# Second mixer of a two-layer diffusion trunk: state sums and state products as three products of rounded halves, both scan directions merged into one mixing matrix

## The reference

```python
def ssd_chunk_scan(xs, dt, A, Bm, Cm, h0):       # L = 128 tokens a chunk, two chunks
    xdt = xs * dt;  a = dt * A
    def step(state, inp):
        xc, ac, bc, cc = inp
        cs = jnp.cumsum(ac, axis=1)
        seg = jnp.where(lower, cs[:, :, None] - cs[:, None, :], -jnp.inf)
        w = jnp.einsum('blgn,bsgn->blsg', cc, bc)[..., None] * jnp.exp(seg)
        y = jnp.einsum('blsgk,bsgkp->blgkp', w, xc)
        y = y + jnp.einsum('blgn,bgkpn->blgkp', cc, state) * jnp.exp(cs)[..., None]
        tail = jnp.exp(cs[:, -1:] - cs)[..., None]
        state = state * jnp.exp(cs[:, -1]) + jnp.einsum('bsgn,bsgkp->bgkpn', bc, xc * tail)
        return state, y

for d, rev in ((0, False), (1, True)):           # forwards and backwards
    yc_d, hc_d = ssd_chunk_scan(f(xc), f(dtc[:, :, d]), A[d], f(Bc), f(Cc), h0)   # context first
    yl_d, _ = ssd_chunk_scan(f(xl), f(dtl[:, :, d]), A[d], f(Bl), f(Cl), hc_d)    # then the latents
    yl = yl + f(yl_d)
```

## Time and profile before

| | us |
|---|---|
| median of 3 runs (lowest, highest) | 2140.7 (2139.47, 2143.54) |
| the profiled execution's own time | 2139.08 |
| its span | 2137.5 |
| PE busy | 2049.5 (96%) |
| DVE, ACT, POOL busy | 1438.1, 913.5, 776.6 |

### The profile page before, as it was taken

One profiled execution on the slowest core, in us unless ns is written; L12 is line 12 of the kernel. 1 busy time (PEld: TensorE's weight loads), 2 busy tenths in 40 slices (PEclk: granted clock), 3 DMA queues, 4 the chain that ended last, 5 costly groups with the idle time before them and its releaser, 6 DMA issues.

```text
span 2137.5 us, 31164 instructions
## 1 busy us (share of the span) xinstructions
PE 2049.5 (96%) x10694; PEld 1695.5 (79%) x10694; DVE 1438.1 (67%) x1865; ACT 913.5 (43%) x1259; POOL 776.6 (36%) x687
## 2 busy tenths in 40 slices
PE   5989999999999999989988999999999999999997
PEld 2558888888888888768867888888888888887776
DVE  5257777777787777744267767677767667678344
ACT  3244445444455455533354433433443434435433
POOL 1126666666665565645041221221322222222011
PEclk7999999999999999999989999999999999999999
DMA  9976666666676666445434455455454555544653
GB/s 352 361 218 143 184 162 170 171 175 176 174 189 171 169 174 171 137 133 152 111 106 123 127 138 148 118 137 149 106 162 113 142 141 134 127 133 167 239 194 138
DMA packets 417744, 349.21 MB, mean 163 GB/s; under 512 B 13504, under 2 KB 358176, under 8 KB 416544
## 3 DMA queue, kind: packets, MB, share of 16 engines
q1 hardware_dynamic: 392304, 269.76, 43.7%
q0 software_dynamic: 20400, 74.46, 13.8%
q10 hardware_dynamic: 4992, 4.37, 0.7%
HBM read 344.21 MB, written 4.33 MB: 163 GB/s over the span
## 4 chain that ended last, share of the span: by engine, by line
PE 84%; DVE 7%; DMA 3%; ACT 2%; issue 2%; POOL 0%; SPq 0%; DVEq 0%; POOLq 0%; ACTq 0%
PE bank L357 21%; PE bank L361 21%; PE bank L359 21%; PE bank L2104 2%; PE bank L2106 2%; PE bank L2105 2%; PE bank L2034 2%; DMA arena<-in_na_ada_w_dram 2%; DVE w_lo L343 2%; PE bank L2017 1%; PE bank L2027 1%; DVE act_lo L1513 1%; PE bank L1836 1%; PE bank L1810 1%; PE bank L1895 1%
## 5 line engine op out<-in xcount | busy, mean ns | idle before, releaser
L357 PE MATMUL bank<-act_hi,w_hi 128*128 128x512 f32 (+1 forms) x2480 | 916.6, 370 | 22.3 <-DVE w_lo L343 12.3
L361 PE MATMUL bank<-act_hi,w_lo 128*128 128x512 f32 (+1 forms) x2480 | 901.0, 363 | 0.0
L359 PE MATMUL bank<-act_lo,w_hi 128*128 128x512 f32 (+1 forms) x2480 | 900.9, 363 | 0.0
L343 DVE TENSOR_TENSOR w_lo<-arena,w_hi 128x2048 fp32r<-128x2048 f32 x186 | 441.7, 2375 | 182.7 <-ACT w_hi L339 132.7
L357 PEld LDWEIGHTS bank<-act_hi,w_hi 128*128 128x128 f32 x2480 | 471.1, 190 | 100.7 <-DVE w_lo L343 11.6
L361 PEld LDWEIGHTS bank<-act_hi,w_lo 128*128 128x128 f32 x2480 | 470.5, 190 | 73.8
L359 PEld LDWEIGHTS bank<-act_lo,w_hi 128*128 128x128 f32 x2480 | 471.4, 190 | 69.1
L581 POOL TENSOR_TENSOR acc<-acc,arena 128x512 f32<-128x512 f32 x224 | 334.1, 1492 | 123.0 <-ACT arena L830 113.9
L339 ACT ACTIVATE w_hi<-arena 128x2048 fp32r<-128x2048 f32 x141 | 269.2, 1909 | 97.7 <-PE bank L2106 78.2
L1316 DVE SCALAR_TENSOR_TENSOR arena<-arena,cond_c 128x512 f32<-128x512 f32 x240 | 253.3, 1056 | 72.8 <-DMA arena<-in_ssd_ada_w_dram 48.3
L830 ACT ACTIVATE arena<-arena,cond_c 128x512 f32<-128x512 f32 x256 | 171.3, 720 | 283.8 <-POOL acc L581 153.2
(11 more groups left out here) (247 smaller groups left out, 2123.4 us busy)
## 6 DMA issues: line engine op xcount, KB each, us to landing
arena<-in_ssd_w_in_dram SPq DMA_DIRECT2D x81, 1024.0 KB, 6.0
arena<-in_na_w_in_dram SPq DMA_DIRECT2D x58, 1024.0 KB, 7.2
arena<-in_ssd_ada_w_dram POOLq DMA_DIRECT2D x96, 512.0 KB, 4.1
arena<-in_na_ada_w_dram SPq DMA_DIRECT2D x64, 512.0 KB, 8.6
arena<-in_ssd_w_out_dram SPq DMA_DIRECT2D x32, 1024.0 KB, 5.0
arena<-in_na_ada_w_dram POOLq DMA_DIRECT2D x32, 512.0 KB, 4.1
arena<-in_na_w_out_dram SPq DMA_DIRECT2D x16, 1024.0 KB, 6.4
arena<-cs_scr SPq DMA_DIRECT2D x64, 256.0 KB, 5.3
```

Source lines behind the costliest of these rows:

```text
L343: nc.vector.tensor_tensor(w_lo[:, n0 % 2, :], raw[slot], w_hi[:, n0 % 2, :].bitcast(F32), ALU.subtract).then_inc(s_lo, 1)
L357: nc.tensor.matmul(bank[b][:, 0:cols], w_hi[:, b, w], act_hi3[:, k, 0:cols], start=(k == 0), stop=False)
L359: nc.tensor.matmul(bank[b][:, 0:cols], w_hi[:, b, w], act_lo3[:, k, 0:cols], start=False, stop=False)
L361: mm = nc.tensor.matmul(bank[b][:, 0:cols], w_lo[:, b, w], act_hi3[:, k, 0:cols], start=False, stop=(k == KT - 1))
```

## The change

Constants first: `ident` and `ones` share one semaphore, the normalisations share another, and the first norm's product with x runs as four instructions of 2048 columns in place of 16 of 512. In the second mixer:

- `states` and the first part of `products` become three products of rounded halves. For that ACT makes `xdt_hi`, `state_hi`, `b_hi` and `c_hi`, and DVE `xdt_lo`, `state_lo`, `b_lo` and `c_lo`.
- The two directions share one mixing matrix for each head and chunk: `w_cb` is masked C*B times dt, made by ACT for one direction (`cb_by_dt`) and completed by DVE on the diagonal blocks (`cb_diagonals`). POOL multiplies it into `decay` in place, in one instruction. PE then needs four products with the plain turned x (`x_lt`) in place of eight.
- At the start of each group DVE copies the group's scalars to fixed places (`group_columns`).

```diff
+            def cb_by_dt(p, t1, t4):
+                act.wait_ge(s_cbm, t1.at(1))
+                act.wait_ge(s_fg, t1.at(1))
+                if t4.i is not None or p > 0:
+                    act.wait_ge(s_mix, t4.at(p))
+                for hd in range(2):
+                    for st in range(2):
+                        dt = f_g[:, st, st, 2 * p + hd:2 * p + hd + 1]
+                        last = nc.scalar.activation(w_cb[:, hd, st, :], cb_m[:, 384 * st:384 * st + LAT], ACT.Copy,
+                                                    scale=dt)
+                last.then_inc(s_wdt, 1)
...
-                nc.scalar.activation(state, bank[3][:, 0:2 * P], ACT.Copy).then_inc(s_stev, 1)
+                nc.scalar.activation(state_hi, bank[3][:, 0:2 * P], ACT.Copy).then_inc(s_stev, 1)
+
+            def xdt_high(p, t4):
+                act.wait_ge(s_xtmp, t4.at(p + 1))
+                flat = lambda v: v.rearrange("p d t j -> p (d t j)")
+                nc.scalar.activation(flat(xdt_hi), flat(xdt), ACT.Copy).then_inc(s_xhi, 1)
...
                     conv_tanh(2 + j, t6)
+                    if j > 0:
+                        cb_by_dt(j, t1, t4)
                     if j < PAIRS - 1:
                         z_tanh_s(j, t10)
                         hi_s(5 + 2 * j, t10)
...
+                            nc.scalar.activation(c_hi, c_t, ACT.Copy).then_inc(s_btev, 1)
+                        xdt_high(j, t4)
+                        if j == 0:
+                            cb_by_dt(0, t1, t4)
                         decays(j, t4)
...
             def x_weighted(p, t4):
...
-                src = bank[2][:, :].rearrange("p (t h d) -> p t h d", t=4, h=2)
+                src = bank[2][:, 2 * P:4 * P].rearrange("p (t h d) -> p t h d", t=2, h=2)
                 for d in range(2):
-                    f = f_tok[:, :, heads_at(p, t4, 64 * d, 2)].unsqueeze(3).broadcast_to([P, 4, 2, 64])
+                    f = f_g[:, 2:4, d, h:h + 2].unsqueeze(3).broadcast_to([P, 2, 2, 64])
...
+                nc.vector.tensor_copy(x_lt.rearrange("p t d -> p (t d)"), bank[2][:, 0:2 * P])
...
+                dve.wait_ge(s_xhi, t4.at(p + 1))
+                nc.vector.tensor_tensor(flat(xdt_lo), flat(xdt), flat(xdt_hi).bitcast(F32), ALU.subtract)\
+                  .then_inc(s_xdt, 1)
+
+            def state_low(p, t4):
+                dve.wait_ge(s_stev, t4.at(p + 1))
+                nc.vector.tensor_tensor(state_lo, bank[3][:, 0:2 * P], state_hi.bitcast(F32), ALU.subtract)\
+                  .then_inc(s_stlo, 1)
+
+            def group_lows(t2):
+                dve.wait_ge(s_btev, t2.at(2))
+                nc.vector.tensor_tensor(b_lo.rearrange("p a b -> p (a b)"), bank[7][:, 0:2 * P],
+                                        b_hi.rearrange("p a b -> p (a b)").bitcast(F32), ALU.subtract)\
+                  .then_inc(s_glo, 1)
+                nc.vector.tensor_tensor(c_lo, c_t, c_hi.bitcast(F32), ALU.subtract).then_inc(s_glo, 1)
...
+            def cb_diagonals(p, t4):
+                dve.wait_ge(s_wdt, t4.at(p + 1))
+                for hd in range(2):
+                    for st, at in ((0, 640), (1, 256)):
+                        w = w_cb[:, hd, st, P * st:P * st + P]
+                        m = nc.vector.scalar_tensor_tensor(
+                            w, cb_m[:, at:at + P], f_g[:, st, 1 - st, h + hd:h + hd + 1], w,
+                            ALU.mult, ALU.add)
+                m.then_inc(s_wcb, 1)
...
+                    def behind_x(j=j):
+                        if j > 0:
+                            state_low(j - 1, t4)
+                        lo_s(4 + 2 * j, t10)
...
                         x_weighted(j, t4)
                         decay_args(j, t4)
+                        cb_diagonals(j, t4)
+                        if j == 0:
+                            group_lows(Turn() if first else Turn(g, 2))
...
-                for at, size, st, l0 in ((0, 256, 0, 0), (512, 128, 1, 128), (768, 256, 1, 0), (1280, 128, 0, 0)):
-                    last = nc.gpsimd.tensor_tensor(
-                        mix[:, at:at + 2 * size].rearrange("p (h l) -> p h l", h=2),
-                        decay[:, :, st, l0:l0 + size],
-                        cb_m[:, at // 2:at // 2 + size].unsqueeze(1).broadcast_to([P, 2, size]), ALU.mult)
+                pool.wait_ge(s_wcb, turn.at(pair + 1))
+                nc.gpsimd.tensor_tensor(flat, flat, w_cb.rearrange("p h s l -> p (h s l)"), ALU.mult)\
+                  .then_inc(s_mix, 1)
...
-                    mm = nc.tensor.matmul(bank[3][:, 0:2 * P], b_tok[:, t, :], xdt[:, :, 2 + t, :],
-                                          start=(t == 0), stop=(t == 1))
+                    for n, (b, x) in enumerate(((b_hi, xdt_hi), (b_hi, xdt_lo), (b_lo, xdt_hi))):
+                        mm = nc.tensor.matmul(bank[3][:, 0:2 * P], b[:, t, :], x[:, :, t, :],
+                                              start=(t == 0 and n == 0), stop=(t == 1 and n == 2))
...
-                    nc.tensor.matmul(bank[4][:, d * LAT:(d + 1) * LAT], state[:, d * P:(d + 1) * P], c_t,
-                                     start=True, stop=True)
+                    for n, (s, cc) in enumerate(((state_hi, c_hi), (state_hi, c_lo), (state_lo, c_hi))):
+                        nc.tensor.matmul(bank[4][:, d * LAT:(d + 1) * LAT], s[:, mine], cc,
+                                         start=(n == 0), stop=(n == 2))
...
+                for st in range(2):
+                    for hd in range(2):
+                        mm = nc.tensor.matmul(bank[5][64 * hd:64 * hd + 64, 0:LAT], x_lt[:, st, 64 * hd:64 * hd + 64],
+                                              decay[:, hd, st, :], start=(st == 0), stop=(st == 1),
+                                              skip_group_check=True)
```

163 lines of the change are left out of this document (92 added, 71 removed).

## The result

| | before | after |
|---|---|---|
| median of 18 runs each | 2141.01 us | 2148.89 us |
| lowest to highest | 2138.93 to 2144.61 | 2142.68 to 2151.75 |
| profiled execution, span | 2139.08, 2137.5 | 2149.81, 2148.2 |

The prediction said 2151.

What follows compares the result with a forecast made beforehand. PE, busy 96% of the span, was read as the bound before, and a ring of DVE and ACT afterwards. 2139.1 + 8 (groups) + 3 (end) = 2150, stated as 2151 us for the median; range 2134 to 2163.

Steps and rivals of the forecast that it cites:

- What PE saves: Second mixer, per pair: states and state products 0.15 us less each, mixing products 0.48 less, in all 0.78.
- What stands in x_c's way: `state_low` between convolution and w_lo makes x_c 0.34 us later; PE, 0.78 earlier into 0.42 of room, waits.
- The ring: DVE and ACT operations from convolution to convolution, waiting on each other: 21.3 us a pair against 20.43 to 20.58 before.
- C+4.45: C is the end of the convolution; w_lo of the z tile was forecast to start 4.46 us after it, 1.16 later.
- The stall of the first step: POOL's mix product holds the convolution's first step about 0.7 us; the square costs the second 0.3; convolution 4.4 in all.
- One long product is worse than four short ones: POOL's mix beside DVE's convolution: by the skill's exclusion rule, one long product is worse than four short; no separate size.
- A group: Second mixer's groups: first pair +0.05, two full turns and the boundary sum to +1.15 us each, over seven boundaries +8.
- the boundary: From one group to the next: PE starts x0 after waiting for that tile's w_lo, 0.45 us back.
- the full turns: Two in a group, x2 to x3 and x3 to the next B: 0.8 and 0.75 us more.
- The end: Output projection, where PE already waited for DVE: about 3.0 us ahead of y_lo, plus 0.9 lag, less 0.78: +3.
- At nothing: `group_columns`, `group_lows`, `c_hi` and the norm's wide products were costed at nothing; `group_lows` at worst 0.5 us late.
- The clock falls: Rival, chance 0.03: PE idles about 1.5 us a pair; half speed for a tenth of the loop costs some 40.

## Why the prediction was right, and where its terms were off

The direction, the size and the mechanism held: PE's saving did not come through, and a ring of DVE and ACT took over, shown by moving `cb_by_dt` (10 us), by leaving out the halves (16) and POOL's product (19). That the total of 2151 came within 2 us was in part luck: the groups were put at +8 and gave 3, the end at +3 and gave 6.

- **What PE saves.** 0.78 predicted. State products 0.15 (0.96 to 0.81; the prediction had both 0.09 lower, 0.87 and 0.72), mixing products 0.44 in the kernel without halves, and a pair without a wait went from 20.43 to 19.71, 0.72 in all. Right to 0.06.
- **What stands in x_c's way.** PE waits 0.65 at x2 and 0.81 at x3, as said. But `state_low` ahead of x_c is not what makes these waits: without it they stayed (15.6 us in 18 times against 14.4), and x_c ahead of w_lo moved the wait to w_lo.
- **The ring.** w_lo of the z tile came at C+4.45 (4.46 predicted), `x_weighted` took 2.06 (2.03), the decay arguments 2.85 to their end (2.96), the convolution 4.20 (4.4; it was 4.32 in the pair before). Ring 21.03, predicted 21.3. The stall of the first step, 0.60, and of the others, 0.24, were predicted at 0.7 and 0.3.
- **One long product is worse than four short ones**: the prediction drew this from the rule of the Trainium skill (SBUF — State Buffer, "Who interferes with whom") that a VectorE instruction with two SBUF inputs and a GpSimd one that reads SBUF exclude each other. The hold for a whole instruction is there (the first step's work began 0.2 before POOL's end), and the one-operand `tensor_scalar` was held too. The conclusion that pieces would be cheaper for the convolution fell: 4.18 against 4.20.
- **A group.** +1.15 predicted, +0.43 measured. By the table above: x1 to x2 -0.19 instead of +0.05, x2 to x3 +0.42 instead of +0.8, x3 to B +0.53 instead of +0.75, the boundary -0.35 instead of -0.45. The step that failed is the sum of the full turns: the ring was put 0.27 too long in each, and I gave the first pair no share of PE's saving. Seven groups: 3, not 8.
- **The end.** +3 predicted, which held the last group's lag too; in the projection alone it was +6. The idle time at the first tiles was foreseen in kind. What was missed is that the granted clock fell behind 3.16 us of it in one piece, that the wait for the weights at tile 10 grew from 2.09 to 3.73 with the same effect, and that `state_low` and x_c stand behind `state_evac`, which stands behind a w_hi that waits for its DMA: the last turning came 4.7 us later than before, of which 3.6 were there at the last evacuation of x3.
- **At nothing** was wrong for `group_lows`: the subtraction for C took 2.57 in place of 0.34, since POOL's product, from 1478.55 to 1480.94, ran beside it, and PE's products waited 0.3 for it once a group (its weight loads 0.7):

```profile
1478.65 2.57 DVE L1625 TENSOR_TENSOR rounded<-arena,rounded 128x256 fp32r<-128x256 f32 x1
...
1478.55 2.39 POOL L694 TENSOR_TENSOR arena<-arena 128x1024 f32<-128x1024 f32 x1 [4.51 <-ACT arena L1031]
```

- **The clock falls**, a rival at 0.03, came true in a place that it did not name: not in the loop, where no idle time of PE is over 1 us and the clock stays at 1.00, but in the projection, at 1.7 us twice.

## What to carry to other kernels

A saving on the busiest engine is worth what the ring of the others leaves: before replacing one product by three of rounded halves, add up what making the halves costs on the other engines, and where in their queues it stands. An operation whose result is needed only later is free only in a place where its engine waits anyway; the same four Copies cost 10 us more in one place of ACT's queue than in another. And what a wait is put down to is the last of a row of operations: here reordering the row changed only the name of the wait, while shortening it changed the time.

## What the runs showed of the hardware

- Idle POOL is not free capacity beside DVE: a POOL subtraction of 1.29 us made four one-operand DVE instructions, 1.14 together, take 2.21. A POOL product of 1024 columns cost a convolution of four steps 0.82, and four of 256 columns cost 0.80 while lasting 3.29 in place of 2.40. A single subtraction of 0.34 beside the one product took 2.57, beside the four 0.92.
- PE's granted clock fell to its half level behind idle times of 3.16 and 3.73 us in the changed kernel, 0.79 on the mean of 8 us each time, about 1.6 us lost. Behind the second, a record that takes 0.39 elsewhere took 0.63. One idle time alone doesn't say whether it falls: over all traces it fell behind idle times from 1.90 (with one of 2.96 some 6 us before) to 3.90, and stood at 1.00 behind others up to 3.17.
- Six products of rounded halves with 256 columns took 0.81 us from start to start, the two float32 products that they replace 0.96: three for one saves 16%, not a factor.
